# Attention of a hybrid layer: scores recomputed with keys on partitions in place of turned probabilities

## The chip, the cores and the metric

One NeuronCore of a Trainium2 chip (trn2) runs the whole program. The metric is the time that the device reports for one execution, in microseconds (us).

## The reference

The reference is one transformer layer: a mixer with three branches (RWKV-7, an attention with forgetting called fox, and Mamba-2), each gated and merged, then a grouped mixture of experts, with 1024 tokens of width 1024. Only the fox attention is touched here. It has 8 heads of 64, and for a head it computes

```
s = einsum('bqhe,bkhe->bhqk', q, k) * scale + c[query] - c[key]
s = where(key <= query, s, -inf)
o = softmax(s over keys) @ v
```

where c is a cumulative sum of log-sigmoids, one row of 1024 for each head. Everything is in fp32.

## The kernel before, in words

The program is a row of stages with a barrier of all engines between them: `fox_project` makes q, k, v and c, `fox_attend` (line 1470 on) is the attention, `merge_fox` projects its output. q and k have been written to DRAM in two fp32r parts (a rounded high part and the low rest), transposed, with the head's 64 channels on partitions; c likewise as high and low row. V lies in SBUF (`k.fox_v`, a part of the tile `room`), tokens on partitions, in plain fp32. An fp32r product takes one instruction; a product with plain fp32 operands takes two instructions.

`fox_attend` goes through 8 heads of 8 query blocks of 128, one unit u = 8h + i for block i of head h. The engines' programs are written out by hand:

- SP loads a head's eight operands into one of two buffers (line 1523): `q_both` has the high and low part of q on 128 partitions and `k_high` the high part of k twice, so that one product gives high x high and low x high; `q_high` and `k_low` (68 partitions) give high x low and, in four extra rows, c of the query minus c of the key. The loads wait for six constants that VectorE sets first.
- TensorE begins with 32 idle products (`keep_streaming`, line 166) that only keep it busy. `score` (lines 1547 to 1551) makes the scores of a query block, queries on partitions, keys 0 to the diagonal on columns, in pieces of up to 512 columns with two products each, and adds the causal mask by a bf16 product `eye` x `far`. `turn` (lines 1560 and 1565) turns the probabilities block by block, keys on partitions. `times_v` (line 1575) multiplies each turned block with V, 64 columns at a time.
- VectorE takes the row maximum (line 1667), the reciprocal of the row sum (line 1644), copies the first four turned blocks out of PSUM (line 1652) and scales the output by the reciprocal (line 1658).
- ScalarE makes exp(s - maximum) with the row sum as a by-product (line 1624, two instructions) and copies the other turned blocks (line 1612).

In a head TensorE's order for block i is: score of block i + 1, product with V of block i - 1, turn of block i. The first two and the last two heads are written out, the ones between run in a loop. At the end the output, which has queries on partitions, is turned in 32 blocks (line 1601) and copied into `k.fox_oT` (line 1684), which the next stage reads with channels on partitions.

Of the kernel before, what the change touches and what calls it, by code (L numbers as in the profile page):

```python
# [15 lines left out]
P = 128  # L16
# [7 lines left out]
FH = 8  # L24
# [1253 lines left out]
def fox_project(nc, k):  # L1278

    with Space(nc, "fp") as s:  # L1280
# [34 lines left out]
        with s.block() as block:  # L1315
# [69 lines left out]
            def _(act):  # L1385
# [84 lines left out]
def fox_attend(nc, k):  # L1470


    with Space(nc, "fa") as s:

        q_both, k_high = ([s.sb(f"{n}{b}", [P, T], F32R) for b in range(2)] for n in ("q_both", "k_high"))
        q_high, k_low = ([s.sb(f"{n}{b}", [HD + 4, T], F32R) for b in range(2)] for n in ("q_high", "k_low"))
        eye, far = s.sb("eye", [P, P], BF16), s.sb("far", [P, P], BF16)
        p = [s.sb(f"p{b}", [P, T]) for b in range(2)]
        pt = [s.sb(f"pt{b}", [P, NT, P]) for b in range(2)]
        neg_max, total, inv = ([s.sb(f"{n}{b}", [P, 1]) for b in range(2)] for n in ("neg_max", "total", "inv"))  # L1480
        o = k.room[:, 4:8, :].rearrange("p a (b c) -> p (a b) c", c=FH * HD)
        ps_s = [s.ps(f"s{b}", [P, T]) for b in range(2)]
        ps_t = s.ps("t", [P, NT, P])
        ps_o = [s.ps(f"o{b}", [P, HALF]) for b in range(2)]
        loaded = [s.sem(f"loaded{b}") for b in range(2)]
        (consts, scored, max_ready, exp_ready, turned_a, turned_b, a_copied, b_copied, pv_done, inv_ready, o_ready,
         o_turned, o_copied) = (s.sem(n) for n in (
             "consts", "scored", "max_ready", "exp_ready", "turned_a", "turned_b", "a_copied", "b_copied", "pv_done",
             "inv_ready", "o_ready", "o_turned", "o_copied"))


        def units(eng, head):
            head(0, 0)
            head(1, 1)
            with eng.Fori(1, FH // 2 - 1) as r:
                for b in range(2):
                    head(2 * r + b, b)
            head(FH - 2, 0)
            head(FH - 1, 1)

        def before(h, b, i, n):

            return (h, b, i - n) if i >= n else (h - 1, 1 - b, i - n + NT)

        def there(h, i, n):

            return not isinstance(h, int) or NT * h + i >= n

        with s.block() as block:
            @block.sync  # L1510
            def _(sp):
                sp.wait_ge(consts, 6)

                def load(h, b):
                    def part(n, at):
                        return k.fox_qk[n, bass.ds(at, 1)].rearrange("o d s -> (o d) s")

                    for to, src in ((q_both[b][0:HD, :], part(0, h)), (q_both[b][HD:P, :], part(1, h)),
                                    (k_high[b][0:HD, :], part(0, h + FH)), (k_high[b][HD:P, :], part(0, h + FH)),
                                    (q_high[b][0:HD, :], part(0, h)), (k_low[b][0:HD, :], part(1, h + FH)),  # L1520
                                    (q_high[b][HD:HD + 2, :], k.fox_c[:, bass.ds(h, 1)].rearrange("n o s -> (n o) s")),
# [1786 lines left out]
```

## Time and profile before

| | us |
|---|---|
| median of 3 runs | 2597.69 |
| lowest and highest run | 2594.93, 2601.07 |
| the profiled execution, as reported | 2602.09 |
| its span | 2600.4 |
| the attention in it (idle products to last copy) | 829.1 to 1017.4 |
| first score product of the attention | 843.85 |

The profile is of one execution; its times count from the start of its span. PE is TensorE's matrix products and PEld its weight loads, which overlap them, DVE is VectorE, ACT ScalarE, POOL GpSimd, SP the engine that issues most DMAs (SPq is its queue). L1547 is line 1547 of the kernel. A granted clock (PEclk) of 1.00 is TensorE's 2.4 GHz, 0.50 is 1.2 GHz. A product's recorded time includes its way through the array, so what the engine needs for one is read from the distance between two starts.

### The profile page before, as it was taken

The numbers are of one execution on the slowest core, as the hardware profiler recorded it, in microseconds if no ns is written. First come the engines' busy times: TensorE is split into PE (matmuls) and PEld (weight loads), VectorE is DVE, ScalarE is ACT, GpSimd is POOL, SyncE is SP. The second block draws the span as 40 slices with busy tenths as digits, with TensorE's granted clock in tenths as the row PEclk, the third lists the DMA queues.
The fourth block names the chain that finished last, engine by engine and source line by source line (L and its number), as shares of the span: only waits on it lengthen the run. The fifth ranks groups of instructions, "written<-read, shape, count | busy, mean of one in ns | idle before, by whom it ended". The sixth has DMA issues, their size and how long they took to land. (4 is left out here: it accounts for less than half of the span.)

```text
span 2600.4 us, 31858 instructions
## 1 busy us (share of the span) xinstructions
PE 2244.8 (86%) x12096; PEld 1816.1 (70%) x12097; DVE 1293.9 (50%) x1360; ACT 900.1 (35%) x842; POOL 560.8 (22%) x405
## 2 busy tenths in 40 slices
PE   6998699988898998989969979979569999999960
PEld 5666577765587886877858758768557787787750
DVE  1567311114400564114647730335567888888846
ACT  2652111213100332111213321110237777777733
POOL 1222101112420001314535423310012222122102
PEclk9999699999999899999989989989779999999985
DMA  3244433313242332122323221122359999999946
GB/s 111 86 132 128 137 82 95 96 65 139 106 142 55 87 75 90 61 77 81 113 69 106 94 105 49 45 111 81 129 224 384 393 401 386 388 396 384 404 166 267
DMA packets 124739, 425.16 MB, mean 163 GB/s; under 512 B 33440, under 2 KB 54816, under 8 KB 111728
## 3 DMA queue, kind: packets, MB, share of 16 engines
q1 hardware_dynamic: 107072, 355.34, 38.7%
q10 hardware_dynamic: 8272, 35.65, 3.4%
q0 software_dynamic: 9312, 33.04, 3.4%
q8 instruction: 55, 0.90, 0.1%
q14 instruction: 28, 0.23, 0.0%
HBM read 349.86 MB, written 74.12 MB: 163 GB/s over the span
## 5 line engine op out<-in xcount | busy, mean ns | idle before, releaser
L2922 DVE TENSOR_TENSOR ex_sb_low<-landed,high 128x4096 fp32r<-128x4096 f32 x96 | 424.7, 4425 | 122.2 <-ACT high L2863 114.4
L2863 ACT CAST high<-landed 128x4096 fp32r<-128x4096 f32 x93 | 337.7, 3632 | 97.9 <-DMA landed<-exp_gate 51.4
L2779 POOL COPY ex_sb_idx<-slot_token 128x1 uint32 x32 | 70.0, 2187 | 484.6 <-PE ex_ps_x L2801 407.5
L158 PE MATMUL mg_ps_g<-x_high,mg_sb_w_high 128*128 128x512 f32 x384 | 151.8, 395 | 14.2 <-POOL mg_sb_w_low L185 9.3
L159 PE MATMUL mg_ps_g<-x_low,mg_sb_w_high 128*128 128x512 f32 x384 | 150.8, 393 | 0.0
L160 PE MATMUL mg_ps_g<-x_high,mg_sb_w_low 128*128 128x512 f32 x384 | 150.7, 392 | 0.0
L183 POOL CAST mg_sb_w_high<-mg_sb_w 128x1024 fp32r<-128x1024 f32 x24 | 24.9, 1039 | 448.2 <-DMA mg_sb_w<-w_tiles 301.1
L158 PE MATMUL ex_ps_g<-high,ex_sb_xt 128*128 128x512 f32 x256 | 106.3, 415 | 9.7 <-DVE ex_sb_xt L2917 9.5
L158 PE MATMUL ex_ps_y<-high,ex_sb_ht 128*128 128x512 f32 x256 | 104.6, 409 | 9.8 <-DVE ex_sb_ht L2934 9.8
L159 PE MATMUL ex_ps_g<-ex_sb_low,ex_sb_xt 128*128 128x512 f32 x256 | 103.0, 402 | 0.0
L160 PE MATMUL ex_ps_g<-high,ex_sb_xt 128*128 128x512 f32 x256 | 102.8, 402 | 0.0
L158 PE MATMUL ex_ps_u<-high,ex_sb_xt 128*128 128x512 f32 x256 | 101.3, 396 | 1.3 <-DVE ex_sb_low L2922 1.3
L160 PE MATMUL ex_ps_y<-high,ex_sb_ht 128*128 128x512 f32 x256 | 102.0, 398 | 0.0
L159 PE MATMUL ex_ps_y<-ex_sb_low,ex_sb_ht 128*128 128x512 f32 x256 | 101.8, 398 | 0.0
L160 PE MATMUL ex_ps_u<-high,ex_sb_xt 128*128 128x512 f32 x256 | 101.3, 396 | 0.0
L159 PE MATMUL ex_ps_u<-ex_sb_low,ex_sb_xt 128*128 128x512 f32 x256 | 101.2, 395 | 0.0
L1020 DVE TENSOR_TENSOR rc_sb_ab<-rc_ps_m,mats 128x512 f32<-128x512 f32 x32 | 20.6, 686 | 156.3 <-PE rc_ps_m L905 156.3
L158 PEld LDWEIGHTS mg_ps_g<-x_high,mg_sb_w_high 128*128 128x128 f32 x384 | 72.9, 190 | 31.9 <-POOL mg_sb_w_low L185 10.1
L1575 PE MATMUL fa_ps_o<-room,fa_sb_pt 128*128 128x64 f32 (+1 forms) x576 | 78.9, 284 | 12.3 <-ACT fa_sb_pt L1612 9.7
L1575 PEld LDWEIGHTS fa_ps_o<-room,fa_sb_pt 128*128 128x128 f32 x576 | 71.8, 197 | 18.3 <-DVE room L1658 6.2
L160 PEld LDWEIGHTS mg_ps_g<-x_high,mg_sb_w_low 128*128 128x128 f32 x384 | 72.9, 190 | 15.4
L159 PEld LDWEIGHTS mg_ps_g<-x_low,mg_sb_w_high 128*128 128x128 f32 x384 | 73.1, 190 | 15.0
(505 smaller groups left out, 5619.1 us busy)
## 6 DMA issues: line engine op xcount, KB each, us to landing
landed<-exp_gate SPq DMA_DIRECT2D x31, 2048.0 KB
landed<-exp_up SPq DMA_DIRECT2D x31, 2048.0 KB
landed<-exp_down SPq DMA_DIRECT2D x31, 2048.0 KB, 9.7
y_slots<-ex_sb_y ACTq DMA_DIRECT2D x32, 512.0 KB, 10.8
chunk_ch<-slab SPq DMA_DIRECT2D x4, 2048.0 KB
merged_d<-room SPq DMA_DIRECT2D x16, 512.0 KB, 3.0
room<-merged_d ACTq DMA_DIRECT2D x2, 4096.0 KB, 15.7
mg_sb_w<-w_tiles SPq DMA_DIRECT2D x16, 512.0 KB, 3.6
```

What stands on the lines that cost most here:

```text
L158: nc.tensor.matmul(out, lhs[0], rhs[0], start=start, stop=False)
L159: nc.tensor.matmul(out, lhs[0], rhs[1], start=False, stop=False)
L160: return nc.tensor.matmul(out, lhs[1], rhs[0], start=False, stop=stop)
L183: eng.tensor_copy(high, full).then_inc(rounded, 1)
L1020: tt(out[b][:, h:h + 3:2, :], ps_m[o][:, :].rearrange("p (h t) -> p h t", h=2), masks, ALU.mult).then_inc(masked[o], 1)
L1575: m = mm(ps_o[i % 2][:, 0:HD], pt[i % 2][:, j, :], k.fox_v[:, j, bass.ts(h, HD)], start=(j == 0), stop=(j == i))
L2779: nc.gpsimd.tensor_copy(idx[b][:, :], k.slot_token[:, bass.ds(e, 1)]).then_inc(idx_ready, 1)
L2863: nc.scalar.copy(high[part][:, :], k.landed[part][:, :]).then_inc(high_ready[part], 1)
L2922: nc.vector.tensor_tensor(low[part][:, :], k.landed[part][:, :], high[part][:, :], ALU.subtract).then_inc(low_ready[part], 1)
```

## The change

Line numbers are those of the kernel before. `fox_attend` no longer turns the probabilities. For each head it makes the scores twice.

1. `score`: as before with queries on partitions, but in 12 units of at most 512 columns over three PSUM banks (`by_rows`: blocks 0 to 3, then columns 0 to 511 of blocks 4 to 7, then their rest). VectorE takes the negated maximum of each (`reduce`) and, for each half of the queries, joins them and splits them into a high and a low fp32r part (`join`). TensorE turns these into two rows (`turn_max`, four products a half), and ScalarE copies the two rows into partitions 96 and 97 of `q_high` (`keep_max`), against which `k_low` has ones.
2. `score_turned`: the same two products with the roles of q and k exchanged, keys on partitions, so that the maximum is already taken off; 12 units over two banks (`by_keys`: key blocks 0 to 3 for the first half of the queries, 0 to 7 for the second), with a mask `ahead` on the diagonal. ScalarE's exponential of it is already what the product with V needs. There are no turns and no copies of turned blocks, and no row sum.
3. `times_v`: V is the stationary operand, 128 wide: 64 columns of V and 64 columns of ones (set by POOL; V is stored three blocks of 64 to a pair of heads, the middle one being the ones), with up to 512 queries moving, in plain fp32, accumulated over the key blocks in one PSUM bank for each half. The result has channels on 64 partitions and the row sums on the other 64, so it needs no turning at the end.
4. `norm`: VectorE takes the reciprocal of the sums and multiplies, in four pieces of 128 columns for each half. The pieces of a head's second half stand behind the maxima of units 2 to 5 of the head after the next, those of the first half behind units 6 to 9 of the next head.
5. Three buffers for the operands in place of two; the loads start at once, and only the two small loads of a head wait for the rows that VectorE sets. 36 idle products in place of 32. All heads are written out.
6. In `fox_project` ScalarE copies V with gaps for the ones, after waiting for c.

The diff, cut to what carries the change:

```diff
@@ -1399,9 +1399,11 @@
+                act.wait_ge(c_ready, 1)
-                    nc.scalar.copy(k.fox_v[:, n, :], ps_v[n % 2][:, :]).then_inc(v_copied, 1)
+                    nc.scalar.copy(k.fox_v[:, n, :].rearrange("p (a b c) -> p a b c", b=3, c=HD)[:, :, 0:3:2, :],
+                                   ps_v[n % 2][:, :].rearrange("p (a b c) -> p a b c", b=2, c=HD)).then_inc(v_copied, 1)
@@ -1472,218 +1474,223 @@
+        LOW, TOP = HD + 4, 3 * HD // 2 + 2
+        q_both, k_high = ([s.sb(f"{n}{b}", [P, T], F32R) for b in range(3)] for n in ("q_both", "k_high"))
+        q_high, k_low = ([s.sb(f"{n}{b}", [TOP, T], F32R) for b in range(3)] for n in ("q_high", "k_low"))
+        rows = s.sb("rows", [P, TOP - 2 + 2 * NT], F32R)
+        ps_s = [s.ps(f"s{b}", [P, HALF]) for b in range(3)]
+        ps_t = [s.ps(f"t{b}", [P, HALF]) for b in range(2)]
+        by_rows = ([(i, 0, (i + 1) * P) for i in range(4)] + [(i, 0, HALF) for i in range(4, NT)]
+                   + [(i, HALF, (i + 1) * P) for i in range(4, NT)])
+        by_keys = [(0, j, j * P, HALF) for j in range(4)] + [(1, j, max(HALF, j * P), T) for j in range(NT)]
...
+                def load(h):
+                    b = h % 3
...
+                    sp.wait_ge(cleared[b], 3)
+                    for to, src in ((q_high[b][HD:HD + 2, :], k.fox_c[:, h]), (k_low[b][HD + 2:LOW, :], k.fox_c[:, h])):
+                        sp.dma_start(to.bitcast(F32), src).then_inc(loaded[b], 16)
+                for h in range(FH):
+                    if h >= 3:
+                        sp.wait_ge(turned, N * (h - 2))
+                    load(h)
...
+                keep_streaming(nc, k, ps_s[0][:, :], 36)
+                def turn_max(h, half):
+                    pe.wait_ge(max_ready, 2 * h + half + 1)
+                    if 2 * h + half >= 1:
+                        pe.wait_ge(max_kept, 2 * h + half)
+                    for n in range(4):
+                        i = 4 * half + n
+                        m = mm(ps_m[0:TOP, n * P:(n + 1) * P], rows[:, 2 * i:2 * i + TOP], ident[:, :], start=True, stop=True)
+                    m.then_inc(max_turned, 1)
+                def score_turned(h, n):
+                    u, b, (half, j, lo, hi) = N * h + n, h % 3, by_keys[n]
+                    if j == 0:
+                        pe.wait_ge(max_kept, 2 * h + half + 1)
+                    if u >= 2:
+                        pe.wait_ge(exp_ready, u - 1)
+                    at, out = slice(j * P, (j + 1) * P), ps_t[n % 2]
+                    mm(out[:, 0:hi - lo], k_high[b][:, at], q_both[b][:, lo:hi], start=True, stop=False, skip_group_check=True)
+                    m = mm(out[:, 0:hi - lo], k_low[b][:, at], q_high[b][:, lo:hi], start=False, stop=(lo != j * P),
+                           skip_group_check=True)
+                    if lo == j * P:
+                        m = mm(out[:, 0:P], eye[:, :], ahead[:, :], start=False, stop=True, skip_group_check=True)
+                    m.then_inc(turned, 1)
+                def times_v(h, n):
+                    u, (half, j, lo, hi) = N * h + n, by_keys[n]
+                    if u == 0:
+                        pe.wait_ge(ones_in, FH // 2)
+                    if j == 0 and h >= 1:
+                        pe.wait_ge(o_ready, 4 * (2 * (h - 1) + half + 1))
+                    at = h // 2 * 3 * HD + h % 2 * HD
+                    mm(ps_o[half][:, lo - half * HALF:hi - half * HALF], k.fox_v[:, j, at:at + P], pt[n % 3][:, 0:hi - lo],
+                       start=(j == 0), stop=(n in (3, N - 1)), skip_group_check=True).then_inc(pv_done, 1)
+                for n in range(N):
+                    score(0, n)
+                    if n == 7:
+                        turn_max(0, 0)
+                for h in range(FH):
+                    for n in range(N):
+                        if n == 2:
+                            turn_max(h, 1)
+                        if h + 1 < FH:
+                            if n == 8:
+                                turn_max(h + 1, 0)
+                            score(h + 1, n)
+                        score_turned(h, n)
+                        if n >= 2:
+                            times_v(h, n - 2)
+                        elif h >= 1:
+                            times_v(h - 1, N + n - 2)
+                for n in range(N - 2, N):
+                    times_v(FH - 1, n)
...
+                def keep_max(h, half):
+                    act.wait_ge(max_turned, 2 * h + half + 1)
+                    nc.scalar.copy(q_high[h % 3][TOP - 2:TOP, half * HALF:(half + 1) * HALF], ps_m[TOP - 2:TOP, :]
+                                   ).then_inc(max_kept, 1)
...
+                for h in range(FH):
+                    for n in range(N):
+                        u, (half, j, lo, hi) = N * h + n, by_keys[n]
+                        act.wait_ge(turned, u + 1)
+                        if u >= 3:
+                            act.wait_ge(pv_done, u - 2)
+                        nc.scalar.activation(pt[n % 3][:, 0:hi - lo], ps_t[n % 2][:, 0:hi - lo], ACT.Exp).then_inc(exp_ready, 1)
+                        if n == 2:
+                            keep_max(h, 1)
+                        if n == 8 and h + 1 < FH:
+                            keep_max(h + 1, 0)
...
+                def reduce(h, n):
+                    _, lo, hi = by_rows[n]
+                    dve.wait_ge(scored, N * h + n + 1)
+                    v.tensor_reduce(most[h % 2][:, n:n + 1], ps_s[n % 3][:, 0:hi - lo], AX.X, ALU.max, negate=True
+                                    ).then_inc(reduced, 1)
...
+                def norm(h, half, part):
+                    o, total = (slice(n % 2 * HD, n % 2 * HD + HD) for n in (h, h + 1))
+                    u, at = 4 * (2 * h + half) + part + 1, slice(part * P, (part + 1) * P)
+                    if part == 0:
+                        dve.wait_ge(pv_done, N * h + (N if half else 4))
+                    v.reciprocal(inv[half][o, at], ps_o[half][total, at]).then_inc(inv_ready, 1)
+                    dve.wait_ge(inv_ready, u)
+                    v.tensor_tensor(k.fox_oT[o, h // 2, half * HALF + part * P:half * HALF + (part + 1) * P], ps_o[half][o, at],
+                                    inv[half][o, at], ALU.mult).then_inc(o_ready, 1)
...
+                for h in range(FH):
+                    for n in range(N):
+                        if h + 1 < FH:
+                            reduce(h + 1, n)
+                        if 2 <= n <= 5 and h >= 1:
+                            norm(h - 1, 1, n - 2)
+                        if n == 3 and h + 1 < FH:
+                            join(h + 1, 0)
+                        if 6 <= n <= 9:
+                            norm(h, 0, n - 6)
+                    if h + 1 < FH:
+                        join(h + 1, 1)
+                for part in range(4):
+                    norm(FH - 1, 1, part)
+                dve.wait_ge(o_ready, 8 * FH)
...
-            k.fox_v = room[:, 0:4, :].rearrange("p a (b c) -> p (a b) c", c=FH * HD)
+            k.fox_v = room[:, 0:6, :].rearrange("p a t -> p (a t)").rearrange("p (b c) -> p b c", b=NT)
```

## Rows read from the trace of the kernel before

**Rows 1.** the page: busy time of each engine over the span
```profile
PE 2244.8 (86%) x12096; PEld 1816.1 (70%) x12097; DVE 1293.9 (50%) x1360; ACT 900.1 (35%) x842; POOL 560.8 (22%) x405
```
**Rows 2.** windows; PE, PEld, DVE, ACT, POOL busy (xcount), PEclk, DMA share, GB/s
```profile
829.00:844.00 15.00, 9.26 (x33) 7.29 (x34) 4.01 (x6) 0.00 (x0) 0.00 (x0) 0.85 0.62 135
844.00:865.00 21.00, 20.58 (x105) 17.99 (x105) 11.54 (x27) 7.04 (x18) 0.00 (x0) 0.62 0.31 69
865.00:984.50 119.50, 109.89 (x840) 97.24 (x840) 74.87 (x195) 48.63 (x123) 0.00 (x0) 1.00 0.35 79
...
1010.00:1018.40 8.40, 6.33 (x33) 4.70 (x33) 5.49 (x9) 0.00 (x0) 0.00 (x0) 0.80 0.00 0
```
**Rows 3.** timeline, 829 to 844 us: start, duration, engine, line, operation
```profile
829.07 9.11 PE L166 MATMUL fa_ps_s<-x_high 128*128 128x512 f32 x32 [2.22 <-PEq L122]
829.30 0.91 DVE L1635 MEMSET fa_sb_q_high<- 4x1024 f32 x1 [34.74 <-PEq L122]
...
833.85 1.17 SPq L1523 DMA_DIRECT2D fa_sb_q_both<-fox_qk  x2
...
843.85 0.44 PE L1547 MATMUL fa_ps_s<-fa_sb_k_high,fa_sb_q_both 128*128 128x128 f32 x1 [5.68 <-issue]
```
**Rows 4.** timeline of DVE: the 128-wide maximum, heads 3 and 4
```profile
904.75 0.28 DVE L1667 TENSOR_REDUCE fa_sb_neg_max<-fa_ps_s 128x1 f32<-128x128 f32 x1
...
924.62 0.29 DVE L1667 TENSOR_REDUCE fa_sb_neg_max<-fa_ps_s 128x1 f32<-128x128 f32 x1
```
**Rows 5.** waits, 866 to 986 us: us in total, times, longest
```profile
DVE fa_sb_pt L1652 <- PE fa_ps_t L1560: 41.8, 46, 2.5
PE fa_ps_o L1575 <- ACT fa_sb_pt L1612: 6.7, 12, 0.7
```
**Rows 6.** timeline of PE: score products, masks, products with V
```profile
916.03 0.28 PE L1549 MATMUL fa_ps_s<-fa_sb_k_low,fa_sb_q_high 68*128 68x256 f32 x1
916.15 0.23 PE L1551 MATMUL fa_ps_s<-fa_sb_far,fa_sb_eye 128*128 128x128 bf16 x1
...
921.26 0.40 PE L1547 MATMUL fa_ps_s<-fa_sb_k_high,fa_sb_q_both 128*128 128x512 f32 x1
921.50 0.39 PE L1549 MATMUL fa_ps_s<-fa_sb_k_low,fa_sb_q_high 68*128 68x512 f32 x1
921.74 0.23 PE L1551 MATMUL fa_ps_s<-fa_sb_far,fa_sb_eye 128*128 128x128 bf16 x1
921.80 1.53 PE L1575 MATMUL fa_ps_o<-room,fa_sb_pt 128*128 x12
```
**Rows 7.** timeline of PE: full fp32 products 512 wide, first merge
```profile
586.77 1.88 PE L1128 MATMUL ro_ps_g<-room,ro_sb_g_up 128*128 128x512 f32 x4
588.49 1.88 PE L1128 MATMUL ro_ps_m<-mixer_oT,mats 128*128 128x512 f32 x4
```
**Rows 8.** groups by form, DVE: shape, xcount, busy us, mean ns, idle before
```profile
L1667 DVE TENSOR_REDUCE fa_sb_neg_max<-fa_ps_s 128x1 f32<-128x512 f32 x8 | 5.5, 692 | 0.4 <-PE fa_ps_s L1551 0.4
L1667 DVE TENSOR_REDUCE fa_sb_neg_max<-fa_ps_s 128x1 f32<-128x384 f32 x8 | 4.4, 552 | 0.5 <-PE fa_ps_s L1551 0.5
L1667 DVE TENSOR_REDUCE fa_sb_neg_max<-fa_ps_s 128x1 f32<-128x128 f32 x8 | 2.3, 283 | 10.9 <-PE fa_ps_s L1551 10.9
L1465 DVE TENSOR_TENSOR dec<-fp_ps_s,cums_tok 128x128 f32<-128x128 f32 x1 | 0.3, 292 | 9.8 <-PE fp_ps_s L1377 9.8
L1644 DVE RECIPROCAL fa_sb_inv<-fa_sb_total 128x1 f32<-128x1 f32 x64 | 9.8, 153 | 0.0
L2654 DVE RECIPROCAL gates<-gates 128x8 f32<-128x8 f32 x1 | 0.2, 203 | 0.0
```
**Rows 9.** groups by form, ACT: the exponential of one 512-wide unit
```profile
L1624 ACT ACTIVATE fa_sb_p<-fa_ps_s,fa_sb_neg_max 128x512 f32<-128x512 f32 x8 | 5.5, 687 | 6.7 <-DVE fa_sb_inv L1644 6.7
```
**Rows 10.** timeline: the turning of the output that closes the attention
```profile
1010.07 6.57 PE L1601 MATMUL fa_ps_t<-mats,room 128*128 128x128 f32 x32 [0.45 <-DVE room L1658]
...
1013.12 4.25 DVE L1684 COPY mixer_oT<-fa_ps_t 128x512 f32<-128x512 f32 x6 [0.36 <-PE fa_ps_t L1601]
```

More of the change, by code:

```diff
@@ L1473, in fox_attend @@
     with Space(nc, "fa") as s:
[L1475 to L1480, printed above, removed]
@@ L1481, in fox_attend @@
-        o = k.room[:, 4:8, :].rearrange("p a (b c) -> p (a b) c", c=FH * HD)
-        ps_s = [s.ps(f"s{b}", [P, T]) for b in range(2)]
-        ps_t = s.ps("t", [P, NT, P])
-        ps_o = [s.ps(f"o{b}", [P, HALF]) for b in range(2)]
[L1485 to L1489, printed above, removed]
@@ L1492, in units @@
[L1492 to L1507, printed above, removed]
+        LOW, TOP = HD + 4, 3 * HD // 2 + 2
@@ new lines, in fox_attend @@
+        q_both, k_high = ([s.sb(f"{n}{b}", [P, T], F32R) for b in range(3)] for n in ("q_both", "k_high"))
+        q_high, k_low = ([s.sb(f"{n}{b}", [TOP, T], F32R) for b in range(3)] for n in ("q_high", "k_low"))
+        eye, far, ahead = (s.sb(n, [P, P], BF16) for n in ("eye", "far", "ahead"))
+        ident = s.sb("ident", [P, P], F32R)
+        most = [s.sb(f"most{b}", [P, 12]) for b in range(2)]
+        neg_max = s.sb("neg_max", [P, 4])
+        rows = s.sb("rows", [P, TOP - 2 + 2 * NT], F32R)
@@ L1511, in _ @@
             def _(sp):
[L1512 to L1521, printed above, removed]
-                                    (k_low[b][HD + 2:HD + 4, :], k.fox_c[:, bass.ds(h, 1)].rearrange("n o s -> (n o) s"))):
-                        sp.dma_start(to.bitcast(F32), src).then_inc(loaded[b], 16)
@@ L1579, in head @@
-                def head(h, b):
-                    for i in range(NT):
-                        if i + 1 < NT:
-                            score(h, b, i + 1)
-                        elif not (isinstance(h, int) and h == FH - 1):
-                            score(h + 1, 1 - b, 0)
-                        if there(h, i, 1):
-                            times_v(*before(h, b, i, 1))
-                        turn(h, b, i)
-                score(0, 0, 0)
-                units(pe, head)
-                times_v(FH - 1, 1, NT - 1)
@@ new lines, in _, with score @@
+                pe.wait_ge(consts, 5)
+                def score(h, n):
+                    u, b, (i, lo, hi) = N * h + n, h % 3, by_rows[n]
+                    if n == 0:
+                        pe.wait_ge(loaded[b], 128 * (h // 3) + 128)
+                    if u >= 3:
+                        pe.wait_ge(reduced, u - 2)
+                    q, out = slice(i * P, (i + 1) * P), ps_s[n % 3]
+                    last = hi == (i + 1) * P
+                    mm(out[:, 0:hi - lo], q_both[b][:, q], k_high[b][:, lo:hi], start=True, stop=False, skip_group_check=True)
+                    m = mm(out[:, 0:hi - lo], q_high[b][0:LOW, q], k_low[b][0:LOW, lo:hi], start=False, stop=not last,
+                           skip_group_check=True)
+                    if last:
+                        m = mm(out[:, hi - lo - P:hi - lo], eye[:, :], far[:, :], start=False, stop=True, skip_group_check=True)
+                    m.then_inc(scored, 1)
@@ L1686, in _ @@
-                dve.wait_ge(o_copied, NT)
+                v = nc.vector
+                for b in range(3):
+                    clear(dve, v.memset, b)
+                    if b == 0:
+                        v.memset(rows[:, :].bitcast(F32), 0.0).then_inc(consts, 1)
+                        v.tensor_copy(eye[:, :], mat(k, "ident")).then_inc(consts, 1)
+                        v.tensor_copy(ident[:, :], mat(k, "ident")).then_inc(consts, 1)
+                        v.tensor_scalar(far[:, :], mat(k, "before"), NEG, None, ALU.mult).then_inc(consts, 1)
+                        v.tensor_scalar(ahead[:, :], mat(k, "before_or_at"), 1.0, -NEG, ALU.subtract, ALU.mult).then_inc(consts, 1)
@@ new lines, in _ @@
+                for n in range(N):
+                    reduce(0, n)
+                    if n == 3:
+                        join(0, 0)
+                join(0, 1)
+                for h in range(FH):
+                    for n in range(N):
+                        if h + 1 < FH:
[8 more added lines that the diff above has]
+                        join(h + 1, 1)
```

163 lines of the change are left out of this document (41 added, 122 removed).

## The prediction, made before the change was built

> **What bounds the kernel now.** The page comes first: TensorE is busy 86% of the span and VectorE 50% [rows 1], an average over a dozen stages, so what this change is worth has to be read in its own stage. The windows over the attention come next. It lasts from 829 to 1018 us, and in the stretch of full heads TensorE is busy 109.9 of 119.5 us while VectorE has 74.9 and ScalarE 48.6 [rows 2]. The start of one head's first maximum to the next is 924.62 - 904.75 = 19.87 us [rows 4]. The waits say the same from the other side: VectorE waits for TensorE's turned blocks (41.8 us), TensorE for others only now and then [rows 5]. So the body is bound by TensorE, eight times some 19.9 us. Around it lie a head and a tail: the first score product runs at 843.85, 10.0 us after the first load is issued at 833.85, which itself waits for VectorE's six constants [rows 3]; and after the last product with V, the output is turned and copied until 1013.12 + 4.25 = 1017.37 [rows 10]. In the first 21 us of the body the granted clock is 0.62, that is mostly the 1.2 GHz level, after 5.7 idle us; later it is at 2.4 GHz [rows 2, 3].
>
> **Prices of TensorE.** A score product 512 wide follows the last by 0.23 us, one 256 wide or less by 0.12, a mask is followed after 0.06 (I take 0.09, since next weights must come in), and the narrow fp32 pieces of the product with V cost (1.53 - 0.28)/11 = 0.114 us each [rows 6]. Full fp32 512 wide is the new form: four instructions in 588.49 - 586.77 = 1.72 us, 0.43 each, two to a product, 0.86 [rows 7]. For 384 columns I scale: 0.17 and 0.65.
>
> **TensorE, a head.** Both scores cover the same 12 units: six 512 wide, two each of 384, 256 and 128. Two products a unit: 12 x 0.23 + 4 x 0.17 + 8 x 0.12 = 4.4 us. Before: 4.4, 8 masks 0.7, 72 pieces with V 8.2, and 36 turns, priced like such a piece, 4.1: 17.4 of the 19.87. After: 4.4 twice, 16 masks 1.4, eight turned maxima 1.0, and V: 6 x 0.86 + 2 x 0.65 + 2 x 0.43 + 2 x 0.23 = 7.8. Sum 19.0 us. The second score and the wide fp32 product eat all that the turns and the narrow products give back; only waits could be won.
>
> **VectorE, a head.** Twelve maxima: 2 x (0.28 + 0.42 + 0.55) + 6 x 0.69 = 6.65 us (0.42 between its neighbours) [rows 8]. The joins are five operations of four columns, 0.15 each as the one-column row has it, 0.8. Copies and scaling go, but eight pieces of reciprocal and multiply come. The multiply (128 columns out of PSUM) is 0.29 [rows 8]. The reciprocal of 128 columns is not in the trace. One column takes 153 ns and eight take 203 ns [rows 8]: 50/7 = 7.1 ns a column, so 0.153 + 127 x 0.0071 = 1.06 us. Lower end: what a multiply of that width takes, 0.29. Upper end: 16 instructions of eight columns, 3.2 us; but the fixed 0.15 is seen in the one-column row, so the slope is nearest. Eight pieces: 8 x 1.35 = 10.8 us, VectorE 18.3 us in all, nearly TensorE's 19.0.
> The same two rows leave the true slope open by a nanosecond or so either way.
>
> **Where they meet.** Neither sum decides, the order does. In iterations 2 to 5 of a head VectorE has a maximum and a piece of the previous head's second half in each, plus a join, and TensorE's first product with V of the second half (iteration 6) waits for the fourth piece, since it starts over in that PSUM bank. VectorE may begin only when score unit 2 is there. Its way: 0.55 + 3 x 0.69 + 4 x (1.06 + 0.29) + 0.3 = 8.3 us. TensorE's way from unit 2 to that wait is its second score 0.3 and V 0.86, iterations 3, 4 and 5 at 1.6, 1.35 and 1.15, and 0.9 of iteration 6: 6.2 us, so it stands still about 2 us a head, with next scores, exponentials and the next products with V queued behind. The ring: 8.3, then TensorE from there to unit 2 of the next head: V 5.2 + 1.3 (with the carried ones), the scores of 7 to 11 and 0 to 2 2.6, turned scores 2.0, masks 1.2, turned maxima 1.0: 13.3. Period 21.6 us against 19.87. ScalarE has 12 exponentials of at most 0.69 and two copies of a two-row tile, some 8 us a head [rows 9]: hidden; without that cover it would cost little, each exponential has an iteration's time.
>
> **Head and tail.** SP no longer waits for constants: its first load goes out at about 829.1 in place of 833.85, the two small ones behind VectorE's first four memsets (to about 833.4, each 0.91 [rows 3]). In order on SP are then six large loads, the wait, two small ones, and the next heads' loads, which are needed 20 us later. With the same 10 us to the first product, 839.2. The idle products, 36 for 32, last to about 829.07 + 9.11 + 4 x 0.23 = 839.1 [rows 3, 6], so TensorE no longer idles there and the clock should still be at 2.4 GHz. POOL's four memsets and the strided copies of V in the stage before (same number of elements) lie beside other work; if not, half a microsecond each. ACT's wait for the cumulative sums was over long before. From 839.2: head 0's scores at VectorE's pace 6.5; first loop, no piece to wait for, 18.5; six loops 129.6; the last without scores 4.4 + 0.7 + 0.5 + 7.8 + 0.7 and a wait of 1, 15.1; then four pieces that nothing hides, 4 x 1.4 = 5.6. End: 839.2 + 175.3 = 1014.5, before 1017.37. The tail of turns (7.3 us) becomes 5.6, the start gives 4.7, the first head at full clock some 2, and 6 x 1.7 = 10 us of that are lost in the ring.
>
> **Sum.** 2.9 us less. The profiled execution reports 2602.09 us (span 2600.4), 4.4 above the median of the runs, 2597.69; so 2599.2 for it, and 2594.8 for the median.
>
> **Rivals.** (a) The reciprocal is cheaper than the slope, 0.85 us a piece if a part of the 50 ns is the reading of strided columns. About 30 pieces lie on the path, so 0.1 us a piece is 3 us: 6 us less, 2588.5. For: one short row carries the slope. (b) It runs like other operations, 0.29: the ring falls below TensorE's 19.0 to 19.2 a head, 6 x 2.4 + 1 + 3.1 = 18.5 less, 2576. Against: eight columns already cost 50 ns more than one. (c) Slower: the pieces hold VectorE longer, and TensorE's wait in iteration 6 grows with them. From 1.33 us a piece (8 us / 30 above mine) the kernel is slower by more than 0.2%; at 1.35, 2603.5. For: source and sums lie in different partitions in PSUM, the rows have SBUF only. (d) A column costs a little over the slope, because 153 ns is what any short operation takes and hides a part of the first column: at 1.2 us a piece, 4.3 us more, 2599.1. For: no row has more than eight columns; against: the slope is what was measured. The Trainium skill ("VectorE: DVE Perf Modes", section "First, the fixed hardware budget") has the reciprocal as an iterative divide with a repeat count of 8; at the 0.96 GHz of its section "Specifications" that would be 8.3 ns a column, and it speaks for this rival; the two rows, at 7.1, agree with it only nearly. (e) The early loads do not help, because the data or the masks arrive as late as before: the 4.7 us are lost, 2599.5; and if the clock falls in the gap, a few more. Against: no load of this stage is issued before 833.85 [rows 3]. It would not do what it says if the waits at the head were simply longer.
>
> **Numbers.** 0.2% is 5.2 us, about what a measurement tells from no change. The forecast has 0.36, reaching from 2590 to 2599 (0.09 of it faster, 0.27 same); (a) 0.20 and (b) 0.06, faster; (c) 0.12, slower; (d) 0.16 (0.14 same, 0.02 slower); (e) 0.10, same. Faster 0.35, same 0.51, slower 0.14. The range 2584 to 2604 leaves out (b), a part of (a) and of (c).
>
> **What would show it.** Right: reciprocals of 1.0 to 1.1 us in the groups; a wait of TensorE for the multiply, about 2 us a head, in the waits; 21.6 us between heads; first score at 839; last multiply near 1014.5. Wrong: heads of 19 us (pieces cheap), of 22 or more (dear); other waits on TensorE, for the exponential or the maximum, longer than a few tenths; fp32 products at other than 0.86.

## The result: slower by 12 us, and the profile after

The changed kernel takes 2609.1 us (median of 14 runs), the kernel before 2597.0 on the same chip: ratio 1.0045, 95% interval 1.0028 to 1.0061. The forecast was 2594.8, 2.9 us faster, with a range to 2604. The sign was wrong, and by 15 us the size. Of all executions in this document one, of the second kernel of run 11, was far slower (3845 us) and is left out of its ratio.

The page of the changed kernel, whose profiled execution has a span of 2607.6 us, beside [rows 1]; an average over the program shows nothing of it:

```profile
PE 2252.4 (86%) x11716; PEld 1786.1 (68%) x11717; DVE 1334.7 (51%) x1371; ACT 892.7 (34%) x794; POOL 563.4 (22%) x409
```

The windows over the attention, beside [rows 2] (busy us and count of PE, PEld, DVE, ACT and POOL, granted clock, DMA share, GB/s):

```profile
828.50:843.30 14.80, 9.77 (x45) 7.68 (x45) 11.91 (x19) 0.00 (x0) 1.90 (x4) 0.94 0.95 205
843.30:859.00 15.70, 15.69 (x52) 11.24 (x53) 8.10 (x19) 2.62 (x5) 0.00 (x0) 0.51 0.54 112
866.00:986.00 120.00, 110.00 (x522) 72.32 (x520) 91.82 (x178) 37.95 (x76) 0.00 (x0) 0.96 0.29 67
1008.20:1030.60 22.40, 15.34 (x70) 9.71 (x68) 16.13 (x28) 6.74 (x14) 0.00 (x0) 0.97 0.00 1
```

One thing stayed that the forecast had gone, and one is new. TensorE runs at the 1.2 GHz level for nearly all of 843 to 859, as it did before [rows 2]; and in the body the mean clock is 0.96 where it was 1.00. The body is still 110 of 120 us busy, but its ten idle us are now one kind of wait (below).

The start of the stage, from the timeline (start, duration, engine, line, operation, idle before and releaser), beside [rows 3]:

```profile
828.47 1.17 SPq L1509 DMA_DIRECT2D fa_sb_q_both<-fox_qk  x2
828.51 8.44 PE L166 MATMUL fa_ps_s<-x_high 128*128 128x512 f32 x36 [2.22 <-PEq L122]
828.75 0.91 DVE L1620 MEMSET fa_sb_k_low<- 32x1024 f32 x1 [34.74 <-PEq L122]
...
834.08 0.91 DVE L1620 MEMSET fa_sb_k_low<- 32x1024 f32 x1 [0.27 <-issue]
...
838.59 0.91 DVE L1620 MEMSET fa_sb_k_low<- 32x1024 f32 x1 [0.16 <-issue]
838.59 0.30 PE L1534 MATMUL fa_ps_s<-fa_sb_k_high,fa_sb_q_both 128*128 128x128 f32 x1 [1.64 <-DMA fa_sb_k_low<-fox_c]
...
842.02 0.91 DVE L1624 MEMSET fa_sb_k_low<- 2x1024 f32 x1 [0.27 <-issue]
842.97 1.09 DVE L1647 TENSOR_REDUCE fa_sb_most<-fa_ps_s 128x1 f32<-128x128 f32 x3
843.31 0.80 PE L1534 MATMUL fa_ps_s<-fa_sb_k_high,fa_sb_q_both 128*128 128x512 f32 x1 [3.38 <-DVE fa_sb_most L1647]
```

The first load and the first score product come as forecast, the product 5.3 us earlier than before. The idle products end 1.64 us ahead of it, at 836.95, and TensorE waits for the small load of c. The real trouble is that VectorE is not there: it clears all three sets of buffers, twelve memsets of 0.91 us, and the third set begins at the very moment of the first score. TensorE fills its three score banks and stands still 3.38 us until the first maximum has freed one. In this gap the granted clock falls to 0.5, and it stays there until 858.7. The windows of one us at both ends (the third number from the right is the granted clock):

```profile
841.00:842.00 1.00, 0.00 (x0) 0.00 (x0) 0.76 (x1) 0.00 (x0) 0.00 (x0) 0.79 1.01 217
...
858.00:859.00 1.00, 1.00 (x3) 0.50 (x2) 0.00 (x0) 0.43 (x1) 0.00 (x0) 0.68 0.00 0
```

The start and the body, beside [rows 4]: the timeline of DVE, first maximum of heads 1 to 5.

```profile
853.24 0.28 DVE L1647 TENSOR_REDUCE fa_sb_most<-fa_ps_s 128x1 f32<-128x128 f32 x1
...
874.02 0.29 DVE L1647 TENSOR_REDUCE fa_sb_most<-fa_ps_s 128x1 f32<-128x128 f32 x1
...
896.91 0.29 DVE L1647 TENSOR_REDUCE fa_sb_most<-fa_ps_s 128x1 f32<-128x128 f32 x1
...
920.27 0.29 DVE L1647 TENSOR_REDUCE fa_sb_most<-fa_ps_s 128x1 f32<-128x128 f32 x1
...
941.54 0.29 DVE L1647 TENSOR_REDUCE fa_sb_most<-fa_ps_s 128x1 f32<-128x128 f32 x1
```

Heads 2 to 4 take 22.89, 23.36 and 21.27 us (the next two 23.37 and 21.24), against 19.87 before: not one length but several. The waits of 866 to 986 us, beside [rows 5], name what stands ahead of them:

```profile
PEld fa_ps_o L1574 <- issue: 12.0, 5, 2.7
PE fa_ps_o L1574 <- DVE mixer_oT L1671: 10.0, 5, 2.3
```

Once a head TensorE waits some 2 us for the multiply that ends the fourth piece. What follows such a wait is in the timeline of PE and in the windows of one us each:

```profile
882.83 0.39 PE L1560 MATMUL fa_ps_t<-fa_sb_q_high,fa_sb_k_low 98*128 98x512 f32 x1
885.04 1.14 PE L1574 MATMUL fa_ps_o<-fa_sb_pt,room 128*128 128x512 f32 x2 [1.82 <-DVE mixer_oT L1671]
885.57 1.04 PE L1534 MATMUL fa_ps_s<-fa_sb_k_high,fa_sb_q_both 128*128 128x512 f32 x1
...
887.68 1.86 PE L1574 MATMUL fa_ps_o<-fa_sb_pt,room 128*128 128x512 f32 x2
```

```profile
884.00:885.00 1.00, 0.00 (x0) 0.00 (x0) 0.97 (x3) 0.00 (x0) 0.00 (x0) 1.00 0.00 0
...
886.00:887.00 1.00, 1.00 (x4) 0.81 (x3) 0.77 (x2) 0.00 (x0) 0.00 (x0) 0.50 0.06 16
```

The engine is idle at full clock and busy again at half: a product with V 512 wide, which is two instructions, takes 1.14 and then 1.86 us. The waits are 1.82 and 2.28 us in turn (a seventh, in the last head, is 0.79 us). The clock falls after four of the six, for about 3.4 us each time, in the three heads of 22.9 to 23.4 us and in the last.

The forms of DVE, beside [rows 8], give the prices:

```profile
L1669 DVE RECIPROCAL fa_sb_inv<-fa_ps_o 64x128 f32<-64x128 f32 x64 | 61.1, 955 | 6.3 <-PE fa_ps_o L1574 4.4
L1647 DVE TENSOR_REDUCE fa_sb_most<-fa_ps_s 128x1 f32<-128x512 f32 x48 | 33.0, 688 | 15.0 <-PE fa_ps_s L1538 12.2 <-PE fa_ps_s L1535 2.1
L1671 DVE TENSOR_TENSOR mixer_oT<-fa_ps_o,fa_sb_inv 64x128 f32<-64x128 f32 x64 | 18.5, 289 | 2.2
```

And the tail, beside [rows 10]: four pieces that nothing hides, 5.2 us, of which the timeline's first and last are

```profile
1024.36 0.95 DVE L1669 RECIPROCAL fa_sb_inv<-fa_ps_o 64x128 f32<-64x128 f32 x1 [2.96 <-PE fa_ps_o L1574]
...
1029.29 0.29 DVE L1671 TENSOR_TENSOR mixer_oT<-fa_ps_o,fa_sb_inv 64x128 f32<-64x128 f32 x1
```

The stage ends at 1029.58, where it ended at 1017.37: it is long enough by itself for the whole loss of 12 us. (The two profiled executions differ by only 7.2 us, because the rest of the program happened to be 5.6 shorter in the second; see run 1.)

### The profile page after: what moved, and what is told of

It reads as the page before. It is cut to its first block and busy times, and to the rows that moved or that the text cites. A ratio compares the mean times of both kernels' runs of the same rounds, so it can differ in the third digit from the quotient of the medians.

```text
span 2607.6 us, 30468 instructions
## 1 busy us (share of the span) xinstructions
PE 2252.4 (86%) x11716; PEld 1786.1 (68%) x11717; DVE 1334.7 (51%) x1371; ACT 892.7 (34%) x794; POOL 563.4 (22%) x409
## 5 line engine op out<-in xcount | busy, mean ns | idle before, releaser
L2786 POOL COPY ex_sb_idx<-slot_token 128x1 uint32 x32 | 62.2, 1943 | 490.4 <-PE ex_ps_x L2808 413.0
L1574 PE MATMUL fa_ps_o<-fa_sb_pt,room 128*128 128x512 f32 (+1 forms) x192 | 85.6, 530 | 13.1 <-DVE mixer_oT L1671 13.1
L1613 ACT ACTIVATE fa_sb_pt<-fa_ps_t 128x512 f32<-128x512 f32 (+1 forms) x96 | 47.1, 490 | 117.7 <-PE fa_ps_t L1563 71.3
```

The source lines that it names most:

```text
L1574: mm(ps_o[half][:, lo - half * HALF:hi - half * HALF], k.fox_v[:, j, at:at + P], pt[n % 3][:, 0:hi - lo], start=(j == 0), stop=(n in (3, N ...
L1613: nc.scalar.activation(pt[n % 3][:, 0:hi - lo], ps_t[n % 2][:, 0:hi - lo], ACT.Exp).then_inc(exp_ready, 1)
L2786: nc.gpsimd.tensor_copy(idx[b][:, :], k.slot_token[:, bass.ds(e, 1)]).then_inc(idx_ready, 1)
```

## The experiments

Stages start at other times in other executions, so I compare stage lengths: from the stage's first load (before: from its idle products, 829.07) to the subtraction that opens the merge on VectorE. It was 190.9 us before (to 1019.96) and 203.7 after (828.47 to 1032.20). Each stage length is of one profiled execution; the ratios are of all. A fall below is a stretch at the 1.2 GHz level, and a head's length is from its first maximum to the next head's. Dots in a diff stand for lines left out. Ratios are to the kernel before on the same chip, 95% interval in brackets.

**1. The clears alone.** GpSimd does sets 1 and 2, ScalarE waits for each set where it writes it first.

```diff
+                for b in (1, 2):              # GpSimd, each memset waited for
+                    clear(pool, nc.gpsimd.memset, b)
...
-                for b in range(3):
+                for b in range(1):            # VectorE
                     clear(dve, v.memset, b)
```

> GpSimd clears buffers 1 and 2 in place of VectorE, ScalarE waits for each buffer's clears only where it first writes it. Theory C (VectorE's eight further clears hold its first maximum until 842.97): the first maximum starts at about 838.9, right behind the first score product; the stall of 3.4 us goes, and with it the half clock of 841.8 to 858.7 if TensorE then has work: 4 us less for the stall alone, 7 with the clock, so 2605 to 2602 us against the changed kernel's 2609. Rival (data or masks arrive late, or the first head is slow for another reason): the first maximum moves, but head 1's first maximum stays at 853.2 and the time at 2609.

Measured: 0.9984 (0.9969 to 0.9999), stage 193.2 us. The timeline of DVE in this run, whose first load is at 832.43:

```profile
842.86 2.14 DVE L1657 TENSOR_REDUCE fa_sb_most<-fa_ps_s 128x1 f32<-128x128 f32 x4 [4.19 <-PE fa_ps_s L1539]
...
850.52 0.29 DVE L1657 TENSOR_REDUCE fa_sb_most<-fa_ps_s 128x1 f32<-128x128 f32 x1
...
869.05 0.29 DVE L1657 TENSOR_REDUCE fa_sb_most<-fa_ps_s 128x1 f32<-128x128 f32 x1
```

VectorE now waits for the first score (4.19 us) and not the other way round. Head 1's first maximum is 18.1 us behind the first load, where it was 24.8, and head 2's 36.6 against 45.6: 9 us, all at full clock. The clears are the cause, and not the loads: here too TensorE waits for the small load of c ahead of the first score (1.42 us), and nothing comes of it. Heads of 22.9 and 23.35 us remain further on, with falls. The ratio fell by more than the stage shows (16 us against 10.5); what lies outside the stage took 2395 to 2416 us in the traces of this study, so a difference of some 5 us between a profile and a median stays unexplained here, and one of 4 to 8 in runs 3 and 4; the intervals of two ratios together allow some 5.5.

**2. How much of the start is the clock.**

```diff
-                keep_streaming(nc, k, ps_s[0][:, :], 36)
+                keep_streaming(nc, k, ps_s[0][:, :], 52)
```

> 52 idle products ahead of the first score product in place of 36: 16 x 0.234 = 3.7 us more, so the scores start at 842.3 in place of 838.6, when VectorE is still at its clears (to 842.9). Theory C: the scores were too early by those 3.7 us, so nothing is lost; TensorE no longer stands still 3.4 us and keeps 2.4 GHz through the first head and a half (in the changed kernel half clock from 841.8 to 858.7): head 1's first maximum comes 24.8 - 2.5 = some 22.3 us after the first load, 2 to 3 us less, 2606. Rival (the half clock has nothing to do with the gap): head 1's first maximum stays at 24.8, same time. Rival (start of the scores counts): 3.7 more.

Measured: 1.0018 (1.0000 to 1.0035), stage 196.0 us. Head 1's first maximum is 21.8 us behind the first load (853.51 - 831.73), head 2's 39.4 (871.13). The window from 845 to 860, all half clock in the changed kernel:

```profile
845.00:860.00 15.00, 14.69 (x84) 10.38 (x82) 11.00 (x27) 3.51 (x8) 0.00 (x0) 1.00 0.64 137
```

The first maximum comes 14.5 us behind the first load in both kernels (846.23 - 831.73, 842.97 - 828.47), and the scores begin 3.4 us later here (845.29 is 13.56 us behind the load, 838.59 was 10.12); yet the start is 6.2 us shorter. So of the 9 us, 6 are the clock and 3 the late maximum: theory C, with a larger clock term than I expected.

**3. The bank.** The piece keeps its length; only who holds the PSUM bank changes.

```diff
-                        pe.wait_ge(o_ready, 4 * (2 * (h - 1) + half + 1))
+                        pe.wait_ge(o_kept, 2 * (h - 1) + half + 1)
...
+                    nc.scalar.copy(kept_o[half][:, :], ps_o[half][:, :]).then_inc(o_kept, 1)
...
-                    v.reciprocal(inv[half][o, at], ps_o[half][total, at])
+                    v.reciprocal(inv[half][o, at], kept_o[half][total, at])
```

> ScalarE copies each finished half of the product with V out of PSUM (one copy of 512 columns, some 0.7 us), TensorE waits for that copy, and VectorE's reciprocals and multiplies read the copy: same number and length of pieces. Theory R (TensorE stands still because the fourth piece holds the PSUM bank of the second half, and its clock falls in that wait): TensorE's wait for the multiply goes, no half clock between 870 and 1000, heads of 19.2 to 19.6 us, about 7 x 2 + 8 = 22 us less and 0.7 more at the tail: 2588. Rival V (VectorE's work for a head, 18 to 20 us with its waits, sets the pace, whoever holds the bank): the wait moves to the maxima, heads stay near 21, 2600 to 2609. Rival P (TensorE's own two scores and wide fp32 products fill the head): heads stay at 21.2 to 23.4, 2609.

Measured: 0.9959 (0.9946 to 0.9973), stage 185.7 us. The same 120 us as above:

```profile
866.00:986.00 120.00, 120.00 (x596) 80.20 (x595) 100.81 (x200) 50.39 (x99) 0.00 (x0) 1.00 0.29 67
```

TensorE never stops in it and the clock never falls; from head 3 on a head takes 19.33 to 19.45 us. Head 2 shows 21.19, and in run 11, with a fast start, 21.21; but TensorE starts its scores of heads 2 and 3 only 19.23 us apart (872.29, 891.52), and it is VectorE that falls from 0.7 to 2.7 us behind them there. VectorE has 100.8 us of work and holds nobody up: theory R, and rivals V and P fall. A reciprocal that reads SBUF takes 947 ns, against 955 from PSUM, so where the sums lie costs nothing.

**4. No division.**

```diff
-                    v.reciprocal(inv[half][o, at], ps_o[half][total, at])
+                    v.tensor_copy(inv[half][o, at], ps_o[half][total, at])
```

> Each reciprocal piece is a plain copy of the sums (the division is left out: the output is multiplied by the sums). Theory R and rival V both: a piece shrinks from 0.955 + 0.289 to about 0.6 us, TensorE's wait goes, heads of 19.2 us, the four closing pieces take 2.6 in place of 5.2: 22 + 2.6 = 25 us less, 2584. Rival P: only the tail's 2.6 us go, 2606.

This kernel leaves the division out, so only its time is of use. Measured: 0.9930 (0.9915 to 0.9945), stage 181.6 us, heads of 19.35 and 19.65 from head 2 on. VectorE's work falls from 100.8 us in run 3 to 73.3 and the heads stay where they were: once the wait is gone, a cheaper piece no longer shortens a head. Of the 4.1 us of stage between the two runs 3.8 lie behind the first score of head 7 (40.6 us to the last multiply in run 3, 36.8 here).

**5. Only the clock.**

```diff
+                    if n == 4 and h >= 1:
+                        keep_streaming(nc, k, ps_m[:, :], 8)
                     if j == 0 and h >= 1:
                         pe.wait_ge(o_ready, 4 * (2 * (h - 1) + half + 1))
```

> Eight idle products (8 x 0.234 = 1.87 us) into the bank of the turned maxima, issued by TensorE just before it waits for the fourth piece of the second half, in heads 1 to 7. Theory R with the clock: they run where TensorE stood still for up to 2.3 us, so they cost nothing, the clock stays at 2.4 GHz between 870 and 1000, and every head takes 21.3 us: 8 us less, 2601. Rival (heads of 23.3 us have another cause than the clock, the wait being what the pieces make it): 2609. Rival (TensorE had no such slack): up to 7 x 1.87 = 13 us more, 2622.

Measured: 1.0020 (1.0007 to 1.0033), stage 197.7 us. Full clock throughout the body, heads of 21.2 and 21.65 us in turn. Its wait row for 866 to 986:

```profile
PEld fa_ps_o L1576 <- DVE mixer_oT L1673: 2.5, 5, 0.8
```

56 idle products save 6 us. The heads of 21.2 us are those with the wait of 1.8 us in the changed kernel, those of 21.65 those with 2.3. The row is of the weight loads; the products themselves stand still 0.35 us at most. Since they fill the wait and do not end it, what they save is the wait's after-effect alone.

**6. One reciprocal for a half.** This undoes "in pieces".

```diff
-                        if 2 <= n <= 5 and h >= 1:
-                            norm(h - 1, 1, n - 2)
+                        if n == 2 and h >= 1:
+                            norm(h - 1, 1, 0)         # 512 columns
...
```

> One reciprocal and one multiply of 512 columns for each half of a head, where the first piece stood, in place of four pieces. By the piece's 0.955 us for 128 columns the reciprocal takes some 0.15 + 512 x 0.0063 = 3.4 us, the multiply 0.7: 4.1 us in place of 4 x 1.31 = 5.2, and with no maximum in between the bank is free 4.1 us after the third maximum in place of 8.3, while TensorE gets to it after 6.2. Theory R (order of the pieces among the maxima makes the wait): TensorE's wait for the multiply goes, heads of 19.2 to 19.6 us, no half clock between 880 and 1000: as the freed bank, 18 us and 1 more at the tail, 2590. Rival V (VectorE's work for a head sets the pace): 2.2 us less a head, 21 for 23, 2594 to 2600. Rival W (a block of 4.1 us on VectorE makes TensorE wait for maxima in both halves): heads stay above 21, 2609 or more.

Measured: 0.9962 (0.9947 to 0.9978), stage 183.7 us, heads of 19.5 and 19.63. The one line of it (count, shortest, median and longest ns):

```profile
L1669 DVE RECIPROCAL fa_sb_inv<-fa_ps_o x16: 3350/3355/3360, 859.2 to 1000.2; 64x512 f32<-64x512 f32 x16
```

Undoing the pieces is worth 20 us of stage, the wait and its clock except for 1 us at the tail.

**7. Four pieces, together.** Is it their price or their order?

```diff
-                        if 2 <= n <= 5 and h >= 1:
-                            norm(h - 1, 1, n - 2)
+                        if n == 2 and h >= 1:
+                            for part in range(4):
+                                norm(h - 1, 1, part)
...
```

> Four pieces as in the changed kernel, each 0.955 + 0.289, but all four in one iteration (the third for the second half, the seventh for the first) in place of one in each of four. Same work on every engine, the order of VectorE alone. Theory R (maxima and pieces in turn make the bank free only 8.3 us after the third maximum, and TensorE is there after 6.2): 5.2 us in place of 8.3, so the wait for the multiply goes, no half clock between 880 and 1000, heads of 19.2 to 19.8 us, 18 us less, 2594. Rival (the price of the pieces: they are what the whole reciprocal saved, 1.1 us a half): the wait stays at 1 us or more, heads of 21, 2604 or more.

Measured: 1.0020 (1.0005 to 1.0036), stage 196.7 us, every head some 21.34 us. Neither expectation holds whole: the wait for the multiply is gone, as theory R says, but the heads and the time (1.0020 is 2605 where before is 2600) are as the rival said. The waits of 870 to 990 show where the wait went:

```profile
PEld fa_ps_s L1534 <- DVE fa_sb_most L1647: 16.4, 23, 1.5
PE fa_ps_s L1534 <- DVE fa_sb_most L1647: 8.0, 10, 1.3
```

TensorE has three score banks, and 5.2 us of pieces in one block hold the next maximum longer than those three last. Waits of up to 1.3 us on the products (the PE row), two in most heads, take the place of one of 2.3, and after none of them does the clock fall. A block of 4.1 us (run 6) is short enough. So it is order and price together: spread, the pieces hold the output's bank; in a block, the score's.

**8. The early loads in the kernel before.**

```diff
-                sp.wait_ge(consts, 6)
...
+                        if n == 6 and clears:         # the two small loads
+                            sp.wait_ge(consts, clears)
...
-                keep_streaming(nc, k, ps_s[0][:, 0:HALF], 32)
+                keep_streaming(nc, k, ps_s[0][:, 0:HALF], 36)
```

> The kernel before with one part of the change alone: SyncE's loads of heads 0 and 1 no longer wait for VectorE's constants, only the two small ones of each for its clears, and 36 idle products for 32. VectorE has six constants there, not seventeen, so nothing of it lies before the first maximum. My prediction's step (the early loads are worth 4.7 us, the clock in the first head some 2 more): first score product at about 839.3, 0.9975 of before. Rival (e) of the prediction (data or masks are as late as before): same time as before.

Measured: 0.9962 (0.9949 to 0.9975), stage 179.0 us, 11.9 less than before. The first score comes at 831.95, 9.9 us behind the stage's first idle product, where it was 14.8, and from there to the last copy the clock does not fall:

```profile
845.00:860.00 15.00, 13.66 (x110) 12.31 (x110) 9.08 (x26) 5.59 (x15) 0.00 (x0) 1.00 0.47 108
```

4.9 us come before the first score. The other 7.0 come where the kernel before was at half clock: some 6 up to head 1's first maximum and 1 in the closing turns (half clock from 1010.0 to 1013.4 before, none there in this run). This part of the change is a gain by itself, and the clock is worth over three times what I gave it.

**9. The changed kernel again** (no edit), as control.

> The changed kernel itself, unchanged, beside the next two. By its first measurement 1.0045 of before (1.0028 to 1.0061), so about 2612 where before is 2600. If three to five of its heads again take 23.3 us and the others 21.3, the half clock after the wait is part of every execution; if all heads are 21.3, that was chance of one profile.

Measured: 1.0049 (1.0031 to 1.0067), stage 202.7 us, three heads of 22.89 us in the body and between them two of 21.7. Falls stand in all four traces that have these waits (changed kernel, runs 1, 2 and 9), but not behind the same waits: four of six, and three of six in each of the others. The timeline of PE has the same waits as in the first trace, 1.82 and 2.28 us in turn:

```profile
930.20 1.10 PE L1574 MATMUL fa_ps_o<-fa_sb_pt,room 128*128 128x512 f32 x2 [1.81 <-DVE mixer_oT L1671]
...
953.55 1.10 PE L1574 MATMUL fa_ps_o<-fa_sb_pt,room 128*128 128x512 f32 x2 [2.27 <-DVE mixer_oT L1671]
```

Here the clock falls after the three of 1.8 us (from 887.1, 931.5 and 975.9) and after none of the longer ones; in the first trace it fell after one of 1.82 and all three of 2.28. So the traces price a fall, like beside like: a head with the wait of 1.8 us takes 22.89 with a fall behind it and 21.25 without, one with the wait of 2.3 takes 23.36 and 21.72. A fall costs 1.64 us, about half of the 3.4 us that it lasts.

**10. The account closed:** the edits of runs 1 and 5 together.

> The closing of the account: the changed kernel with the clears of buffers 1 and 2 on GpSimd and eight idle products ahead of TensorE's wait for the fourth piece, so the two terms that the prediction lacks are gone and its ring stays. By the runs so far: first load to head 2's first maximum 18.1 + 18.5 = 36.6 us, five heads of 21.43 (21.2 and 21.65 in turn, as with the idle products alone), 44.5 from head 7's first maximum to the merge's first VectorE operation: 188 us in place of 203.7 in the changed kernel and 190.9 in the kernel before. So 15.5 us less than 1.0047 of before: 0.9988, 2597 where before is 2600, the prediction's 2.9 us less. If a third cost is hidden behind the two, 1.001 or more.

Measured: 0.9991 (0.9974 to 1.0008), stage 188.4 us (829.01 to 1017.38). The same 120 us of the body:

```profile
866.00:986.00 120.00, 118.94 (x583) 81.38 (x581) 96.33 (x184) 39.60 (x79) 0.00 (x0) 1.00 0.29 67
```

With the two terms gone the stage is where the prediction had it: from first load to last multiply 185.7 us (829.01 to 1014.73), forecast 185.4. The ratio alone would not show it. Its interval holds no change at all, and run 1, with the clears alone, has 0.9984 with a stage 4.8 us longer.

**11. Versions that beat both.** Clears on GpSimd with the bank freed (runs 1 and 3), and with the whole reciprocal (runs 1 and 6).

> The clears of buffers 1 and 2 on GpSimd and the bank freed by ScalarE's copy, together. If the two costs are separate, they add: the single runs took 6.7 us off the start (head 1's first maximum 18.1 in place of 24.8 us after the first load) and 18.0 us off the stage with the bank freed, so 24.7 less than the changed kernel's 1.0045: 0.995 of before, 2588 where before is 2600; the head that follows the start may give a part back, since with the bank freed the first head's pace is VectorE's. If they overlap (the late start was paid by the same wait), no better than the bank freed alone, 0.9959.

Measured: 0.9935 (0.9919 to 0.9951), stage 176.0 us.

> One reciprocal of 512 columns for a half, and the clears of buffers 1 and 2 on GpSimd. If the start and the body add: the stage with the whole reciprocal took 183.7 us from first load to the merge's first VectorE operation, less 6.7 for the start: 177.0, by which it would be at 0.9935 or a little under, 2583, with the bank freed and the clears (176.0). If a reciprocal of 3.36 us in the first head holds the scores that now come earlier: 180, 2587.

Measured: 0.9946 (0.9925 to 0.9967), stage 174.4 us. The gains add. The two can't be told apart; the second is the simpler, with no extra buffer or copy, some 14 us below the kernel before.

## Why the prediction was wrong

**What held.** The bound and the order: TensorE's floor was put at 19.0 us a head, and where nothing waits it is 19.3 to 19.65. The ring was put at 21.6, with a wait of 2 us for the fourth piece; heads without a clock fall take 21.2 and 21.7 us in turn. The reciprocal came out 0.955 us (forecast 1.06) and lies on the line through the one-column row [rows 8]: (3.355 - 0.955) / 384 = 6.25 ns a column, 0.155 fixed. Rivals (a) to (d) all turned on that price, and it was not what went wrong: at 0.955 my sum would have come out 0.1 x 30 = 3 us faster still. The Trainium skill ("VectorE: DVE Perf Modes", section "First, the fixed hardware budget") has a repeat count of 8, by which the prediction estimated 8.3 ns a column at 0.96 GHz. The 6.25 ns do not bear that estimate out; the measurement decides. First score 838.6 (839.2), the two instructions of a wide fp32 product 0.43 to 0.48 us apart (0.43), tail 5.2 (5.6): right or nearly.

**What failed, first: "Head and tail".** It counted VectorE's first four memsets for SyncE's sake and then let the scores of head 0 run at VectorE's pace from 839.2. The other eight, 0.91 us and a gap each, were in the diff and their price was in [rows 3], but the prediction follows only who waits for a clear, not what stands behind it on its own engine. From first load to head 2's first maximum I had 35.1 us (829.1 to 864.2); it took 45.6, and without the clears 36.6. Of the 9 us, 6 came by the clock. The sentence that "the clock should still be at 2.4 GHz" looked at the gap ahead of the first score and not at the one behind it. The gap ahead was not quite gone either: 36 idle products took 8.44 us, not 10.0, since the 9.11 us of the 32 before were in part at half clock (0.85 in [rows 2]). That did no harm: run 9's first score follows the idle products without a gap, and its clock falls all the same, behind a wait of 3.66 us for the first maximum.

**Second: "Where they meet".** The wait was priced at its own length. The prediction speaks of the clock behind the 5.7 idle us at the head [rows 2, 3], but not behind the 2 us that it puts into every head. Four of six waits were followed by 3.4 us at the 1.2 GHz level, 1.64 us each: 6.6. Run 5, which fills the waits, gave 6.0. The Trainium skill ("TensorE: Matmul & The Clock Gate", section "HAM oscillation — how this bites in real kernels") describes a kernel that falls back to half rate at each wait between its tiles; this trace agrees in part, with a fall after four of its six waits, once a head, and with shorter waits (1.82 and 2.28 us).

**The sum.** The stage ended 15.1 us later than forecast (1029.58 against 1014.5), and the two terms, 9 and 6 to 6.6, make that up. In stretches: up to head 2's first maximum 10.4 more than forecast (45.55 against 35.1), from there to the last multiply 5.3 more (155.6 against 150.3), and the first load went out 0.6 earlier. With both terms out (run 10) these stretches are 36.2 and 149.5. So the start has still 1 us more than its forecast and the rest 1 us less, and that the sum then meets it within 0.3 us is in part luck. The ratio, 0.9991, agrees with the forecast's 0.9989 (2594.8 over 2597.7) more closely than its interval can tell. The prediction's own balance at the end of "Head and tail" does not add up to its sum: 1.7 at the tail, 4.7 and 2 at the start, less 10 in the ring, is 1.6 us slower, not 2.9 faster; the forecast rests on the chain of 175.3 us alone.

**The rivals.** Slower had 0.14, nearly all of it rival (c), a dearer piece; the kernel is slower with a cheaper one. Rival (e) came nearest, the early loads lost and the clock falling, but it blamed the data and the masks. In truth the loads' gain is real (run 8), and the same change buries it under its own clears. Of the signs of being wrong, "heads of 22 or more (dear)" came true with a cheap piece: it is the clock that makes them.

## What to carry to other kernels

When a wait is moved away from the head of a stage, list every instruction of every engine up to its first part in the loop; the constants that nobody waits for are still ahead of somebody's first work. Price a wait of TensorE at its length and what the clock does afterwards, and look for the waits that recur once a period. Before cutting an operation into pieces between others, ask which buffer stays held until the last piece; the whole operation, or a cheap copy by an idle engine that frees the buffer, may be the shorter hold.

## What the runs showed of the hardware

- In the body the granted clock fell after single waits of 1.8 and 2.3 us, four of six in one trace and three of six in another, and not always after the longer ones (run 9). After waits of up to 1.3 us (run 7) it did not fall. It fell only once the engine was at work again: resumed at 885.04, half clock from 886.0. Each of these falls lasted 3.4 us and cost 1.64. The gap of 2.2 us ahead of the stage's idle products was followed by such a fall in ten of the 14 traces.
- At the start of the stage the fall came inside the gap, of 3.4 us (changed kernel) or 5.7 us (before), and lasted 17 us though TensorE was busy 15.69 of 15.70 us. The runs don't show why one fall lasts 3.4 us and another 17, nor which wait is hit.
- A clear of 1024 columns takes VectorE 0.91 us, over 2 partitions, 32 or 34.
- The reciprocal is linear from 1 to 512 columns, about 0.155 us + 6.25 ns each (the rows: 0.153 for 1, 0.203 for 8, 0.955 for 128, 3.355 for 512), and costs the same out of PSUM and SBUF (955 and 947 ns).
